# Prompt attention of a hybrid decoder: two branches in two halves of the matmul array, gates applied to the outputs

## The reference, cut to what matters

```python
s_c = q . kv_cmp_k * scale + bias      # keys compressed by 16: at most 63
s_s = q . k_slc * scale + bias         # all keys up to the query (all 16 blocks of 64 are chosen)
s_w = q . k_win * scale + bias         # the last 512 keys
p_c, p_s, p_w = masked_softmax(s_c), masked_softmax(s_s), masked_softmax(s_w)
o = gate_c * (p_c . v_cmp) + gate_s * (p_s . v_slc) + gate_w * (p_w . v_win)
```

## Time and profile before

| | |
|---|---|
| three runs | 4792.4, 4794.13, 4809.37 us; median 4794.13 |
| profiled execution | 4797.22 us, of which its span 4795.4 |
| mean granted clock of TensorE | 0.901 |
| TensorE busy | 4076.8 us (85%) |
| VectorE, ScalarE, GpSimd busy | 1961.7 (41%), 1275.3 (27%), 684.0 (14%) us |
| prompt's attention, layer 0 | about 891 to 1226 us of the span |
| prompt's attention, layer 1 | about 3232 to 3551 us |

### The profile page before, as it was taken

The page is one execution under the profiler, slowest core; times in us unless marked ns, Lnnn a source line. Parts: engine busy times, 40 slices in busy tenths (PEclk is TensorE's granted clock), DMA queues, the critical chain, the costliest instruction groups (busy, mean ns, idle before and its releaser), DMA issues. The chain is left out here.

```text
span 4795.4 us, 58781 instructions
## 1 busy us (share of the span) xinstructions
PE 4076.8 (85%) x23204; PEld 3406.5 (71%) x23204; DVE 1961.7 (41%) x3875; ACT 1275.3 (27%) x2922; POOL 684.0 (14%) x495
## 2 busy tenths in 40 slices
PE   3899797787697799989969997967759789999897
PEld 2899676433465799987759996753336579999774
DVE  1333476523244433334442436763324353333354
ACT  0211255222222212113331114532212222121232
POOL 0035101233120000000000540013322010000000
PEclk9999899567798899999989998976879799999998
DMA  3334311300433222225532433121034222222554
GB/s 130 118 131 151 109 56 41 102 3 4 153 156 123 77 67 76 70 70 216 190 118 97 151 125 91 59 70 48 4 117 175 90 98 71 67 80 58 187 179 146
DMA packets 303623, 488.71 MB, mean 102 GB/s; under 512 B 64008, under 2 KB 234024, under 8 KB 298687
## 3 DMA queue, kind: packets, MB, share of 16 engines
q1 hardware_dynamic: 298730, 417.75, 26.9%
q0 software_dynamic: 4608, 67.11, 3.5%
HBM read 382.48 MB, written 117.95 MB: 104 GB/s over the span
## 5 line engine op out<-in xcount | busy, mean ns | idle before, releaser
L791 PE MATMUL ps<-h_hi,fu_hi 128*128 128x344 f32 x2112 | 680.5, 322 | 6.2 <-DVE fu_lo L831 6.2
L793 PE MATMUL ps<-h_hi,fu_lo 128*128 128x344 f32 x2112 | 676.6, 320 | 0.0
L792 PE MATMUL ps<-h_lo,fu_hi 128*128 128x344 f32 x2112 | 675.2, 320 | 0.0
L322 PE MATMUL ps<-zi_whi,h_hi 128*128 128x374 f32 x1440 | 487.0, 338 | 20.5 <-DVE h_lo L417 20.5
L323 PE MATMUL ps<-zi_wlo,h_hi 128*128 128x374 f32 x1440 | 482.6, 335 | 0.0
L324 PE MATMUL ps<-zi_whi,h_lo 128*128 128x374 f32 x1440 | 481.7, 335 | 0.0
L791 PEld LDWEIGHTS ps<-h_hi,fu_hi 128*128 128x128 f32 x2112 | 397.3, 188 | 9.4 <-DVE fu_lo L831 6.4
L793 PEld LDWEIGHTS ps<-h_hi,fu_lo 128*128 128x128 f32 x2112 | 398.6, 189 | 0.0
L792 PEld LDWEIGHTS ps<-h_lo,fu_hi 128*128 128x128 f32 x2112 | 397.3, 188 | 0.0
L946 PE MATMUL ps<-fd_whi,fd_fhi 128*128 128x512 f32 (+1 forms) x792 | 313.2, 395 | 41.7 <-DVE fd_flo L998 41.3
L947 PE MATMUL ps<-fd_wlo,fd_fhi 128*128 128x512 f32 (+1 forms) x792 | 311.6, 393 | 0.0
(11 more groups left out here) (589 smaller groups left out, 6945.4 us busy)
## 6 DMA issues: line engine op xcount, KB each, us to landing
fd_raw<-w_ffn_down SPq DMA_DIRECT2D x66, 1024.0 KB, 5.4
z<-zi_z SPq DMA_DIRECT2D x180, 187.0 KB, 1.9
zi_raw<-w_in SPq DMA_DIRECT2D x20, 1496.0 KB, 6.8
n_x<-z SPq DMA_DIRECT2D x64, 384.0 KB, 4.8
f_all<-fu_f SPq DMA_DIRECT2D x44, 516.0 KB, 3.4
fu_raw<-w_ffn_gate SPq DMA_DIRECT2D x44, 512.0 KB, 4.6
fu_raw<-w_ffn_up SPq DMA_DIRECT2D x44, 512.0 KB, 5.9
fd_f<-f_all SPq DMA_DIRECT2D x44, 384.0 KB, 3.3
```

The lines of the kernel that those rows point to most:

```text
L322: nc.tensor.matmul(out, rows_hi, w_hi[:, i % 2, k], start=(k == 0), stop=False)
L791: nc.tensor.matmul(out, w_hi[f % 2][:, j, k, :], h_hi[:, k, seg], start=(k == 0), stop=False)
L792: nc.tensor.matmul(out, w_hi[f % 2][:, j, k, :], h_lo[:, k, seg], start=False, stop=False)
L793: m = nc.tensor.matmul(out, w_lo[f % 2][:, j, k, :], h_hi[:, k, seg], start=False, stop=(k == KD - 1))
```

## The change

What it does:

- Keys of the window branch lie on partitions 0 to 63 and those of the selected branch on 64 to 127 of one tensor `kT`. The query is turned two heads at a time, so that head h is on the lower partitions of `qT[:, h]` and on the upper ones of `qT[:, h - 1]`; for the last head 64 columns of the query are loaded a second time behind the others. The compressed keys stay on the lower partitions.
- `scores` puts the matmuls of the two branches in turn: selected, window, selected, window, compressed.
- Blocks are ordered selected, window, selected, window; two of them make a unit. TensorE turns both blocks of unit j (`turns`), then multiplies both of unit j - 1 (`values`). The selected branch is summed in partitions 0 to 63 of bank 6, the window in 64 to 127, the compressed one alone in bank 7.
- Exponentials are no longer scaled: GpSimd has no work in this stage. VectorE makes gate / sum once per row for all heads (`scales`).
- `outputs` turns the sums back (two sets of four transposes) after the first scores of the next quarter, and VectorE multiplies them by gate / sum and adds the three branches, four instructions. SyncE's store waits for the last of them.
- VectorE's copies of turned blocks are no longer linked.

```diff
-        self.kTs = sb("p_kTs", [HD, SEQ])
-        self.kTw = sb("p_kTw", [HD, SEQ])
-        self.qT = sb("p_qT", [HD, H, SEQ])
+        self.kT = sb("p_kT", [P, SEQ])
+        self.qT = sb("p_qT", [P, H, SEQ])
...
-        self.zq = sb("p_zq", [P, NT, 256])
+        self.zq = sb("p_zq", [P, NT, 320])
...
-    ldq(pd.zq[:], zr[:, NQ:NQ + 256].rearrange("(t p) n -> p t n", p=P))
+    ldq(pd.zq[:, :, 0:256], zr[:, NQ:NQ + 256].rearrange("(t p) n -> p t n", p=P))
+    ldq(pd.zq[:, :, 256:320], zr[:, NQ:NQ + HD].rearrange("(t p) n -> p t n", p=P))
...
-                        pe.wait_ge(S("q_ld"), 16)
-                    src = pd.zk[:, t, P:P + HD] if kind == 1 else pd.zk[:, t, 256:256 + HD] if kind == 2 else \
-                        pd.zq[:, t, (kind - 3) * HD:(kind - 2) * HD]
-                    m = nc.tensor.transpose(ps[0:HD, g % 3, i * P:i * P + P], src, ident[:])
+                        pe.wait_ge(S("q_ld"), 32)
+                    src = pd.zk[:, t, HD:HD + P] if kind == 1 else pd.zk[:, t, 256:256 + P] if kind == 2 else \
+                        pd.zq[:, t, (kind - 3) * HD:(kind - 1) * HD]
+                    m = nc.tensor.transpose(ps[:, g % 3, i * P:i * P + P], src, ident[:])
...
+            part = slice(HD, P) if kind == 1 else slice(0, HD) if kind == 2 else slice(0, P)
+            dst = pd.cT[:, cols] if kind == 0 else pd.kT[part, cols] if kind <= 2 else pd.qT[:, kind - 3, cols]
...
+            nc.scalar.activation(dst, ps[part, g % 3, :], ACT.Copy, scale=0.125 if kind >= 3 else 1.0).then_inc(S("p_read"), 1)
...
-    def blocks(t):
-
-        nk, w0, nw, ncm = span(t)
-        return [(CC, ncm, vc[0:ncm, :])] + [(i * P, P, zk[:, i, 192:256]) for i in range(t + 1)] + \
-            [(CW + i * P, P, zk[:, w0 // P + i, 320:384]) for i in range(nw // P)]
...
+    def blocks(k):
+
+        t, nk, w0, nw, ncm = span(k)
+        pairs = []
+        for i in range(t + 1):
+            pairs.append((i * P, P, zk[:, i, 192:256], "s", i == 0, i == t))
+            if i < nw // P:
+                pairs.append((CW + i * P, P, zk[:, w0 // P + i, 320:384], "w", i == 0, i == nw // P - 1))
+        return [(CC, ncm, vc[0:ncm, :], "c", True, True)] + pairs
...
+    def units(k):
+
+        return 1 + len(blocks(k)) // 2
+
+    def unit(k, j):
+
+        return range(0, 1) if j == 0 else range(2 * j - 1, min(2 * j + 1, len(blocks(k))))
+
+    def quarter(k, h):
+
+        n = units(k) + 1
+        return range(n * h // 4, n * (h + 1) // 4)
...
-        yT = sb("p_yT", [HD, 512])
-        y = sb("p_y", [P, 2, 256])
+        yT = sb("p_yT", [P, 512])
+        ycT = sb("p_ycT", [HD, 512])
+        ysw = sb("p_ysw", [P, H, 2, HD])
+        y = sb("p_y", [P, 2, H, HD])
         mx = sb("p_mx", [P, 2, H, 3])
         neg = sb("p_neg", [P, 2, H, 3])
         sums = sb("p_sums", [P, 2, H, 3])
-        scl = sb("p_scl", [P, 2, H, 3])
+        scl = sb("p_scl", [P, H, 3])
...
-                def scores(t, h):
-                    nk, w0, nw, ncm = span(t)
-                    if t or h:
-                        pe.wait_ge(S("s_taken"), 4 * t + h)
-                    q = qT[:, h, t * P:t * P + P]
-                    for n0 in range(0, nk, 512):
-                        n = min(512, nk - n0)
-                        nc.tensor.matmul(ps[:, n0 // 512, 0:n], q, kTs[:, n0:n0 + n], start=True, stop=True)
+                def scores(k, h):
+                    t, nk, w0, nw, ncm = span(k)
+                    if k or h:
+                        pe.wait_ge(S("s_taken"), 4 * k + h)
+                    qw = qT[0:HD, h, t * P:t * P + P]
+                    qs = qT[HD:P, (h - 1) % H, t * P:t * P + P]
+                    n = min(512, nk)
+                    nc.tensor.matmul(ps[:, 0, 0:n], qs, kT[HD:P, 0:n], start=True, stop=True)
                     n = min(512, nw)
-                    nc.tensor.matmul(ps[:, 2, 0:n], q, kTw[:, w0:w0 + n], start=True, stop=True)
+                    nc.tensor.matmul(ps[:, 2, 0:n], qw, kT[0:HD, w0:w0 + n], start=True, stop=True)
+                    if nk > 512:
+                        nc.tensor.matmul(ps[:, 1, 0:nk - 512], qs, kT[HD:P, 512:nk], start=True, stop=True)
                     if nw > 512:
-                        nc.tensor.matmul(ps[:, 3, 0:P], q, kTw[:, w0 + 512:w0 + nw], start=True, stop=True)
-                    nc.tensor.matmul(ps[:, 3, P:P + ncm], q, kc[0:HD, 0:ncm], start=True, stop=True).then_inc(S("scored"), 1)
-
-                def values(t, i):
-
-                    g = first[t] + i
-                    bl = blocks(t)
-                    col, n, v = bl[i]
-                    taken(pe, g)
-                    m = nc.tensor.matmul(ps[0:HD, 6 + t % 2, :], v, pT[0:n, g % 4, :], start=(i == 0), stop=(i == len(bl) - 1))
-                    if i == len(bl) - 1:
-                        m.then_inc(S("y_summed"), 1)
-
-                def turn(t, i):
-
-                    g = first[t] + i
-                    bl = blocks(t)
-                    if g >= 2:
-                        taken(pe, g - 2)
-                    if i == len(bl):
-                        pe.wait_ge(S("yT"), t + 1)
+                        nc.tensor.matmul(ps[:, 3, 0:P], qw, kT[0:HD, w0 + 512:w0 + nw], start=True, stop=True)
+                    nc.tensor.matmul(ps[:, 3, P:P + ncm], qw, kc[0:HD, 0:ncm], start=True, stop=True).then_inc(S("scored"), 1)
...
+                def turns(k, j):
+                    bl = blocks(k)
+                    for i in unit(k, j):
+                        g = first[k] + i
+                        if g >= 2:
+                            taken(pe, g - 2)
+                        if i == 0:
+                            pe.wait_ge(S("exped"), 4 * k + 4)
+                        col, n = bl[i][:2]
                         for h in range(H):
-                            m = nc.tensor.transpose(ps[:, 4 + g % 2, h * HD:h * HD + HD], yT[:, h * P:h * P + P], ident[0:HD, 0:HD])
-                    else:
+                            m = nc.tensor.transpose(ps[0:n, 4 + g % 2, h * P:h * P + P], s[:, k % 2, h, col:col + n], ident[:])
+                        m.then_inc(S("turned"), 1)
...
+                def values(k, j):
+                    bl = blocks(k)
+                    for i in unit(k, j):
+                        g = first[k] + i
+                        col, n, v, kind, start, stop = bl[i]
+                        taken(pe, g)
+                        dst = ps[0:HD, 7, :] if kind == "c" else ps[0:HD, 6, :] if kind == "s" else ps[HD:P, 6, :]
+                        m = nc.tensor.matmul(dst, v, pT[0:n, g % 4, :], start=start, stop=stop)
...
+                def outputs(k):
+                    g = first[k + 1] - 2
+                    taken(pe, g - 2)
+                    pe.wait_ge(S("ycT"), k + 1)
+                    for h in range(H):
+                        m = nc.tensor.transpose(ps[:, 4 + g % 2, h * HD:h * HD + HD], ycT[:, h * P:h * P + P], ident[0:HD, 0:HD])
+                    m.then_inc(S("turned"), 1)
+                    taken(pe, g - 1)
+                    pe.wait_ge(S("yT"), k + 1)
+                    for h in range(H):
+                        m = nc.tensor.transpose(ps[:, 4 + (g + 1) % 2, h * P:h * P + P], yT[:, h * P:h * P + P], ident[:])
                     m.then_inc(S("turned"), 1)
 
                 for h in range(H):
                     scores(0, h)
-                for t in range(NT):
-                    nb = len(blocks(t))
+                for k in range(NT):
                     for h in range(H):
-                        if t + 1 < NT:
-                            scores(t + 1, h)
-                        for g in quarter(t, h):
-                            i = g - first[t]
-                            if i < nb:
-                                turn(t, i)
-                            if 0 < i:
-                                values(t, i - 1)
-                            if i == nb:
-                                turn(t, i)
+                        if k + 1 < NT:
+                            scores(k + 1, h)
+                        if k and h == 0:
+                            outputs(k - 1)
+                        for j in quarter(k, h):
+                            if j < units(k):
+                                turns(k, j)
+                            if j:
+                                values(k, j - 1)
+                outputs(NT - 1)
...
-                def scale(t, h):
-                    nk, w0, nw, ncm = span(t)
-                    dve.wait_ge(S("exped"), 4 * t + h + 1)
-                    k = t % 2
-                    link(V.reciprocal(scl[:, k, h, :], sums[:, k, h, :]))
-                    link(V.tensor_tensor(scl[:, k, h, :], scl[:, k, h, :], ng[:, t, h, :], ALU.mult))
-                    link(V.tensor_tensor(scl[:, k, h, 0:1], scl[:, k, h, 0:1], valid[:, t:t + 1], ALU.mult), S("scales"))
...
+                def scales(k):
+                    t = ORDER[k]
+                    dve.wait_ge(S("exped"), 4 * k + 4)
```

(65 more changed lines are left out.)

96 lines of the change are left out of this document (41 added, 55 removed).

## The result

Four runs of the changed kernel gave 4589.16 to 4601.96 us, median 4595.65, beside 4796.01 for the kernel before (four runs on the same chip): ratio 0.9577, 95% interval 0.9554 to 0.9601. The later runs were taken in batches on different chips, where the kernel before had medians of 4789 to 4799 us; between runs of two batches a difference of ten us says little.

The account below looks back on a forecast made before the run. No engine is full in the prompt's attention; TensorE's work and the chain through VectorE and ScalarE bound it. Stages falling from 325.3 to 267 us per layer save 117, less 3 for the load: 4680 us, range 4615 to 4755.

Parts of the forecast that it names:

- Scores, side by side: Attention scores: n alternating matmuls cost n + 1 passes, not 2n; row 6 takes 1.8 us at high clock, not 2.94.
- Values: Value matmuls of a two-block unit: three passes if column halves overlap, 1.35 us plus 0.1 at high clock; four if not.
- U: TensorE's turnings and values for one two-block unit: 2.5 us high, 4.7 low; 2.95 and 5.6 without overlap.
- The sum: Attention stage per layer: 219 us all high, 320 all low, 267 taken with about half the work at each level.
- The other edits: GpSimd's scaling gone: row 7's 6.36 us wait and shorter ones; later outputs: 0.77 wait gone, 0.6 of transposes added per row.
- E: Rival: halves take turns and each change drains the array; scores +36, values +14 per layer; 4830 us, slower; chance 0.05.
- The chain L: Long quarters: scores to value matmul through maxima, exponentials and ScalarE's copy; 3.5 us for row 0 to 5.7 for row 6.
- The second query load: Extra 256 KB query load before attention: nothing to 3 us per layer, 1.5 taken, 3 us in all.
- B: Rival: column halves of the value matmuls don't overlap; 14 us per layer, 4708 us; chance 0.17.
- C: Rival: the clock stays low through the attention stage; 320 us per layer, 4789 us, no change; chance 0.08.
- F: Rival: score passes of 512 columns don't overlap, no drain; +36 us per layer, 4752 us; chance 0.05.
- D: Rival: the clock stays high for nearly all of the attention stage; 235 us per layer, 4617 us; chance 0.10.

Follow-up runs that it names:

- The grouped order: Changed kernel with score matmuls ordered selected, selected, window, window, compressed, halves kept: 4599.05 us, ratio 0.9588.
- copy-first: Changed kernel with ScalarE copying the first turned block before the next row's exponentials in quarters 1 to 3: 4511.43 us, ratio 0.9412.
- the late one: Changed kernel with ScalarE's copy before the exponentials, and the scores of rows 3 to 7 only in one half: 4595.88 us, ratio 0.96.
- The run without halves: Changed kernel with all scores in one half and values of one branch after another, overlap left for 5 pairs per layer: 4710.83 us, ratio 0.9818.

## Why the prediction was wrong

The sign, the place and the overlap of halves held; the size did not. The gain was 203 us in the two stages, and 117 were forecast: 43 more per layer. By the forecast's own sum two terms made the difference, each about half. The runs allow a second split of the same 43, which shows a third term that was too low.

**"Scores, side by side" and "Values": the count of passes.** The step that failed is "only neighbours of different halves can overlap ... n alternating matmuls cost n + 1 passes". I read the earlier trace rows rightly for whether halves overlap and took the order of the program for the order of the passes. The right count is the longer half alone. Row 7's scores 1.91 (forecast 2.0), row 6's 1.70 (1.8), rows 3 to 5 1.20 to 1.48 (1.6 to 1.8); a pair of value matmuls 1.01 (1.45), so U = 2.03 high (2.5) and 3.8 low (4.7). The forecast's own sums with these values give some 203 all high and 293 all low, in place of 219 and 320. At the forecast's share of low clock (267 lies 48% of the way) that is 246, not 267: about 21 us per layer. The grouped order shows the count directly. The values' part is bounded by the run with values of one branch after another: without their overlap the kernel loses 17 us in all, since most of it lies beside the chain.

**"The sum": about half the work at each level of the clock.** Measured 222 and 226: (222 - 203) / (293 - 203) = 21% and 25% of the work at the low level. That is the other 22 us per layer. The granted clock gives nearly the same: a mean of 0.81 is 38% of the time low, and at half speed that is 23% of the work. By the same estimate the kernel before had 47% in layer 0 (0.68) and 32% in layer 1 (0.76): "about half" was layer 0's share, taken for both, and the earlier trace rows had the other.

My reason was half of the truth. Long waits do cost the clock: the stretch with the waits of up to 3.8 us stands at 0.75, of the eight first turnings after a wait of 2.7 to 3.8 us in the two layers six take longer than 1.09 us, up to 1.97, and when copy-first takes the waits away the last rows stand at 1.00. But the level in the stretches without such waits is set by something I took as given. From 914 to 950 us the runs with all scores in two halves stand at 0.81 (one block to a unit) to 1.00, those with all or the early rows' in one half at 0.50 to 0.70, though TensorE is idle for longer in the former; the kernel before stands at 0.59. One place doesn't fit: the late one scores row 2 in two halves, and in layer 0 its clock was still 0.50 to 0.70 there (not so in layer 1, by the length of the row). One half costs 62 us per layer where its passes ask for 27 at the high clock, and in copy-first 61. The rest is the clock, and this second effect of the change was missing from my sum. That the scores' two halves bring it is shown by four runs (all or some rows in one half, in two orders). What in them does it is not: with the values serial too the clock was higher (0.74, not 0.64) with more work, so no simple tally of work explains it, and it stays open.

**"The other edits": too low.** The forecast's prices for the halves, 36 and 14 per layer (E), leave 8 of its 58 for all the rest (14 by its own lengths of the scores, which give 20 high and 40 low, not 36). The run without halves puts the rest at 44 and the halves, with what they do to the clock, at 58. So seen from the runs most of the surplus is in units, order and the absence of GpSimd. The forecast counted row 7's 6.36 "and shorter ones", and the 0.77 waits; the waits for GpSimd alone came to 19.1 and 17.7 us in the two layers, eight in each. How the 44 divides among the other edits stays open: they were not taken back one by one, but for GpSimd (+12) and the units (+73, with the values' overlap in it).

**Point by point besides.**
- The chain L: right. In the long quarters of rows 5 and 6 the waits are 2.7 to 3.8 us, forecast L - U = 3.2. With 29.7 us in layer 0 ScalarE's copy is the largest idle item, and row 6, forecast 46, took 48.6 since its quarters mix levels. The run with ScalarE's copy first shows what it was worth: 84 us.
- GpSimd: back in the path it costs only 12 us, and row 7 has no wait for it. The waits for it, 19.1 and 17.7 us in the kernel before, are 1.8 in each layer with it back. So its absence is not what gained them, but that it no longer waits for reciprocals and that the outputs are turned later.
- Row 7, forecast 27 at mixed clock (23 high), took 18.7: all high, and five pairs at 2.03 (2.4 less); 2 us less than these two explain.
- Outputs: VectorE's products after the maxima cost TensorE a wait of up to 2.5 us in quarter 0, 11.0 us in layer 0, where I had them beside ScalarE's exponentials. That term was too low; moving them ahead, though, costs more than they do (+30).
- The second query load: 0.3 to 0.4 us per layer, not 1.5.
- The rivals: B (column halves don't overlap) fell; +17 is its price by measurement, 28 as forecast. C fell. E and F fell: changes of half cost nothing seen, and passes of 512 overlap. D (235 per layer, 4617) named the right direction of the clock with the wrong count, and still lay 21 us above the time. The range's lower end was D with my count; the bounds of the pass count should have been in it.

## What to carry to other kernels

When two streams of matmuls go to different halves of the array, count each half as its own queue and take the longer; the two orders tried between them cost the same. Before a forecast, add up all waits that an edit removes from the list of waits, not only the longest. Price the TensorE clock as part of the change, from rows on either side, and keep both ends of it in the range: here, by the forecast's sum, it was half of the surprise. After a change that shortens TensorE's work, look at who hands it the next tile: putting ScalarE's copy before its exponentials gave 84 us more (4511.4 us, ratio 0.9412, the fastest version run), and was worth 70 in the kernel before as well, so it had been there to find.

## What was not expected of the hardware

- Starts are out of program order, and not only by whole instructions: L2334's passes start at 1068.78 and 1068.84, before the second of L2331 at 1068.98, which the program has first.
- The signal of an end keeps the order. One semaphore, on L2334, tells VectorE that a head's scores are there, L2331's too. L2334's own end is modelled at 1069.11, but VectorE starts at 1069.64, 0.14 after TensorE has gone on from L2331 to the next matmul. With all scores in one half, where the compressed scores do come last, VectorE starts 0.04 us after their end. In the changed kernel it is so in every head of rows 5 to 7, in both layers: VectorE starts 0.06 to 0.16 us after the modelled end of the last pass of the longer half, and in rows 6 and 7 that is 0.33 to 1.11 after L2334's. So a single semaphore was enough here. The timelines of VectorE in the changed kernel, and of both in copy-first with one half:

```profile
1069.64 0.26 DVE L2405 CUSTOM_DVE_ANT_0 p_s<-ps,p_T 128x63 f32<-128x63 f32 x1 [2.85 <-PE ps L2334]
```

```profile
1115.19 0.33 PE L2335 MATMUL ps<-p_kc,p_qT 64*128 64x63 f32 x2
...
1115.56 0.26 DVE L2406 CUSTOM_DVE_ANT_0 p_s<-ps,p_T 128x63 f32<-128x63 f32 x1 [3.48 <-PE ps L2335]
```

- Even the transposes of the outputs, which read the lower partitions alone, start beside the other half's last pass. The rows from layer 0, low clock: L2367 at 1044.97, the pass of L2331 at 1045.07.

```profile
1044.65 0.52 PE L2334 MATMUL ps<-p_kc,p_qT 64*128 64x63 f32 x2
1044.97 0.31 PE L2367 MATMUL ps<-ident,p_ycT 64*128 64x64 f32 x1
1045.07 1.06 PE L2331 MATMUL ps<-p_kT,p_qT 64*128 64x512 f32 x1
```

- A TensorE that is 95% busy (34.3 of 36 us) stood at 0.50 for the whole stretch, and one that was 83% busy in the same stretch of time at 0.91. A low clock was not carried into later rows.
